# State-space stage of a two-block network: four groups one after the other, against three interleaved chains

## The reference

```
# 32 heads of 64 in 4 groups; sequence 512 in 4 chunks of 128; state size 128
cb      = C @ B^T                                  # once per group and chunk
decay   = exp(a_cum[l] - a_cum[s]), causal         # per head
y_diag  = (cb * decay) @ (x * dt)                  # "own" chunk
states  = B^T @ (x * dt * decay_to_end)            # per group and chunk, carried on
y_off   = (C @ state_before) * exp(a_cum)          # "past" chunks
y       = y_diag + y_off + d_skip * x
y       = rmsnorm_per_group(y * silu(z)) * gain    # over the 512 channels of a group
merged  = sigmoid(g_att) * (att @ w_att_out) + sigmoid(g_ssm) * (y @ w_ssm_out)
x       = x + merged @ w_out
```

## Time and profile before

| | |
|---|---|
| median of 3 runs | 2856.41 us (2852.3 to 2861.36) |
| the profiled execution | 2849.98 us, of which 2848.2 us is the span |
| granted TensorE clock over the span | 0.962 of full |
| PE busy | 2662.3 us (93%) |
| DVE, ACT, POOL busy | 1448.1, 663.1, 1142.3 us |
| state-space stage | 2050.46 to 2412.64 us, 362.2 us |

### The profile page before, as it was taken

The page is one execution under the profiler, slowest core; times in us unless marked ns, Lnnn a source line. Parts: engine busy times, 40 slices in busy tenths (PEclk is TensorE's granted clock), DMA queues, the critical chain, the costliest instruction groups (busy, mean ns, idle before and its releaser), DMA issues.

```text
span 2848.2 us, 30951 instructions
## 1 busy us (share of the span) xinstructions
PE 2662.3 (93%) x11724; PEld 2070.7 (73%) x11724; DVE 1448.1 (51%) x1985; ACT 663.1 (23%) x1297; POOL 1142.3 (40%) x764
## 2 busy tenths in 40 slices
PE   8999899999999999999999999999888778899998
PEld 6888688888666578888876777766555546688886
DVE  4754574565544435546566744544334447555521
ACT  2004420111233312102132133322213232222200
POOL 4333355555312145555544533322222113455554
PEclk9999999999899999999999999999888879999999
DMA  6433465656312156565644744434433214465565
GB/s 200 125 115 123 129 192 194 193 194 195 122 60 76 43 167 190 194 195 189 210 156 152 229 148 154 157 126 133 159 123 117 96 45 140 146 195 194 191 195 168
DMA packets 148857, 436.62 MB, mean 153 GB/s; under 512 B 13872, under 2 KB 18160, under 8 KB 148720
## 3 DMA queue, kind: packets, MB, share of 16 engines
q1 hardware_dynamic: 64224, 200.29, 23.9%
q0 software_dynamic: 67584, 201.35, 20.2%
q10 hardware_dynamic: 16912, 33.14, 3.2%
HBM read 417.90 MB, written 16.83 MB: 153 GB/s over the span
## 4 chain that ended last, share of the span: by engine, by line
issue 38%; PE 32%; POOL 23%; DVE 3%; DMA 2%; ACT 2%; DVEq 1%; ACTq 0%; POOLq 0%; SPq 0%
POOL w_lo L450 18%; PE bank L502 9%; PE bank L504 8%; PE bank L505 8%; POOL w_hi L432 5%; PE bank L703 1%; DMA projections<-spill_out 1%; PE bank L1117 1%; PE bank L777 0%; PE bank L780 0%; PE bank L779 0%; DMA residual<-x_in 0%; PE bank L1077 0%; DVE next_gained L2234 0%; PE bank L1107 0%
## 5 line engine op out<-in xcount | busy, mean ns | idle before, releaser
L450 POOL TENSOR_TENSOR w_lo<-w_raw,w_hi 128x1024 fp32r<-128x1024 f32 x376 | 908.9, 2418 | 15.1 <-DMA w_hi<-stream 7.1
L432 POOL DMA_DIRECT2D w_hi<-stream x376 | 227.2, 604 | 1673.1 <-PE bank L502 1505.4
L502 PE MATMUL bank<-x_hi,w_hi 128*128 128x512 f32 x1472 | 590.5, 401 | 26.8 <-POOL w_lo L450 13.5
L504 PE MATMUL bank<-x_lo,w_hi 128*128 128x512 f32 x1472 | 578.6, 393 | 0.0
L505 PE MATMUL bank<-x_hi,w_lo 128*128 128x512 f32 x1472 | 578.0, 393 | 0.0
L502 PEld LDWEIGHTS bank<-x_hi,w_hi 128*128 128x128 f32 x1472 | 279.8, 190 | 96.9 <-issue 20.9
L505 PEld LDWEIGHTS bank<-x_hi,w_lo 128*128 128x128 f32 x1472 | 279.6, 190 | 59.7
L504 PEld LDWEIGHTS bank<-x_lo,w_hi 128*128 128x128 f32 x1472 | 279.9, 190 | 57.5 <-issue 2.4
L1983 DVE TENSOR_TENSOR relu_sq<-relu 128x512 f32<-128x512 f32 x64 | 179.1, 2799 | 94.6 <-ACT relu L1395 94.6
L502 PE MATMUL bank<-hidden_hi,w_hi 128*128 128x512 f32 x512 | 199.2, 389 | 0.0
L504 PE MATMUL bank<-hidden_lo,w_hi 128*128 128x512 f32 x512 | 199.2, 389 | 0.0
(11 more groups left out here) (435 smaller groups left out, 4450.8 us busy)
## 6 DMA issues: line engine op xcount, KB each, us to landing
w_hi<-stream POOLq DMA_DIRECT2D x376, 512.0 KB, 4.8
w_raw<-stream SPq DMA_DIRECT2D x376, 512.0 KB, 3.7
projections<-spill_out ACTq DMA_DIRECT2D x56, 256.0 KB, 2.0
ssm_x<-projections ACTq DMA_DIRECT2D x4, 1024.0 KB, 7.2
gate_tiles<-projections ACTq DMA_DIRECT2D x16, 256.0 KB, 3.2
ssm_z<-projections ACTq DMA_DIRECT2D x4, 1024.0 KB, 9.5
residual<-x_in SPq DMA_DIRECT2D x4, 512.0 KB, 10.7
toeplitz_hi<-toeplitz_rows_hi POOLq DMA_DIRECT2D x4, 512.0 KB, 6.5
```

The source lines that it names most:

```text
L432: e.dma_start(in_slot(whi, t % SLOTS, o), in_stream(o)).then_inc(hi_ready[t % SLOTS], 16)
L450: e.tensor_tensor(wlo[:, s, :], raw[:, s, :], whi[:, s, :].bitcast(F32), ALU.subtract).then_inc(lo_ready, 1)
L502: mm = e.matmul(out, wh, rh, start=first, stop=False)
L504: e.matmul(out, wh, rl, start=False, stop=False)
```

## The change

The slots are replaced by one loop over the 16 head pairs in which three chains lie side by side on each engine: the pair itself; the preparation of the next group (`PREP_AT`: transposes T0 to T2 in pair 1, T3, B and the first state S0 in pair 2, S1 and S2 in pair 3); and the end of the group in front with its output units (`E_UNITS`, keys (g, p, place 1 to 3)). Only group 0 is prepared on its own ("first"). For that, `ssm_x_nat`, the states and B's copy are doubled, y has a buffer of its own, exp of the decay rows, y's high half, z and the gates have fewer buffers. x of group 0 is loaded some steps before the projections end. No arithmetic is added or removed.

```diff
@@ placing
+HEAD_STEPS = [(g, p) for g in range(4) for p in range(4)]
+PREP = ["T0", "T1", "T2", "T3", "B", "S0", "S1", "S2"]
+PREP_AT = {1: ["T0", "T1", "T2"], 2: ["T3", "B", "S0"], 3: ["S1", "S2"]}
...
+        ("first", 0): "a0", ("first", 3): "a1", ("first", 6): "a2",
+        (0, 0, 1): "a3", (0, 1, 1): "a4", (0, 2, 1): "a5", (0, 3, 1): "a6", (1, 0, 1): "a7",
+        (1, 2, 2): "o00", (1, 2, 3): "o01", (1, 3, 1): "o02", (1, 3, 2): "o03 o04", (2, 0, 1): "o05 o06",
+        (2, 0, 2): "o07",
...
+        ("last", 0): "o24 o25", ("last", 1): "o26 o27", ("last", 2): "o30 o31 o32 o33 o34 o35 o36 o37"}.items():
@@ PE
+                for g, p in HEAD_STEPS:
+                    n = 4 * g + p
+                    tasks = (PREP_AT.get(p, []) if g < 3 else []) + [None] * 3
+                    rows(n)
+                    units(g, p, 1)
+                    if tasks[0]:
+                        prep(g + 1, tasks[0])
+                    decay_rows(n)
+                    units(g, p, 2)
+                    if tasks[1]:
+                        prep(g + 1, tasks[1])
+                    own_past(n)
+                    if p == 3 and g < 3:
+                        products(g + 1)
+                    if p == 0 and g:
+                        squares_sum(g - 1)
+                    if tasks[2]:
+                        prep(g + 1, tasks[2])
+                    units(g, p, 3)
...
+                            if g == 1:
+                                e.wait_ge(e_add, 3)
+                            elif g:
+                                e.wait_ge(y_rstd, g - 1)
+                        for t in range(4):
+                            mm = e.transpose(bank[4][:, chunk(t)], sx[g % 2][:, t, chunk(c)], ident)
@@ ACT
+                    if n == 61:
+                        e.wait_ge(at_s, n0 + 48)
...
+                        load_x(0)
...
+                for g, p in HEAD_STEPS:
+                    n = 4 * g + p
+                    exponentials(n)
+                    if p == 0 and 1 <= g < 3:
+                        e.wait_ge(sg_yd, 4 * g)
+                        load_x(g + 1)
+                    units(g, p, 1)
+                    if p == 1 and g:
+                        root(g - 1)
+                    past_decay(n)
+                    units(g, p, 2)
+                    if n:
+                        square(n - 1)
+                        if n < 15:
+                            load_z(n + 1)
+                    if p == 2 and g < 3:
+                        natural_b(g + 1)
+                    units(g, p, 3)
+                    if p == 1 and g:
+                        his(g - 1)
@@ DVE
+                    if n:
+                        take_y(n - 1)
+                        gate_y(n - 1)
+                    if p == 2 and g:
+                        low_y(g - 1)
+                    decayed(n)
+                    units(g, p, 1)
+                    if tasks[0]:
+                        prep(g + 1, tasks[0])
+                    units(g, p, 2)
+                    if tasks[1]:
+                        prep(g + 1, tasks[1])
+                    if n:
+                        sum_y(n - 1)
+                    if tasks[2]:
+                        prep(g + 1, tasks[2])
+                    units(g, p, 3)
+                    if p == 1 and g:
+                        norm_y(g - 1)
```

More of the change, by code:

```diff
@@ L1137, in state_space, with units, rows @@
             def state_space():
-                def units(g, name):
-                    for x in E_STEPS[g, name]:
+                def units(*key):
+                    for x in E_UNITS.get(key, []):
                         unit(UNIT_AT[x])
[L1142 to L1159, removed]
+                def rows(n):
                     if n:
@@ new lines, in products, with squares_sum @@
+                def products(g):
+                    for c in range(ST):
+                        mm = e.matmul(bank[5][:, chunk(c)], sb[g % 2][:, chunk(c)], sc[g % 2][:, chunk(c)],
+                                      start=True, stop=True)
+                    mm.then_inc(e_cb, 1)
+                def squares_sum(g):
+                    e.wait_ge(y_sum, 3 * g + 3)
+                    if g < 3:
+                        e.wait_ge(e_add, 3 * (g + 1) + 3)
+                    else:
+                        e.wait_ge(y_rstd, 3)
+                    e.matmul(bank[4][:, :], ones, ysum[:, :], start=True, stop=True).then_inc(y_full, 1)
@@ new lines, in state_space @@
+                for i, task in enumerate(PREP):
+                    prep(0, task)
+                    if i == 0:
+                        products(0)
+                    units("first", i)
+                for g, p in HEAD_STEPS:
[17 more added lines that the diff above has]
+                    units(g, p, 3)
@@ L1234, in state_space @@
+                units("last", 0)
+                squares_sum(3)
+                units("last", 1)
+                units("last", 2)
                 f = flow["w_out"]
@@ new lines, in root, with his @@
+                def root(g):
+                    e.wait_ge(y_full, g + 1)
+                    e.activation(grs[:, :], bank[4][:, :], ACT.Ln, scale=0.25 / 512, bias=col("eps"))
+                    e.drain()
+                    e.activation(grs[:, :], grs[:, :], ACT.Exp, scale=-0.5).then_inc(y_rstd, 1)
+                def his(g):
+                    e.wait_ge(un_full, UNIT_AT["o", g - 1, 7] + 1 if g else UNIT_AT["a", 0, 7] + 1)
+                    for k in range(4):
+                        e.wait_ge(y_n, 4 * g + k + 1)
+                        e.activation(yh[:, k, :], yy[g % 2][:, k, :], ACT.Copy).then_inc(y_hi, 1)
@@ new lines, in state_space @@
+                for k in range(2):
+                    load_z(k)
+                for i, task in enumerate(PREP):
+                    if task == "B":
+                        natural_b(0)
+                    units("first", i)
+                for g, p in HEAD_STEPS:
[18 more added lines that the diff above has]
+                        his(g - 1)
@@ L1707, in state_space @@
+                square(15)
+                units("last", 0)
+                root(3)
+                units("last", 1)
+                his(3)
+                units("last", 2)
                 for m in range(8):
@@ L2300, in by_head, with units, take_y @@
                     return x.rearrange("p (n d) -> p n d", d=64)
[L2302 to L2303 removed]
+                def units(*key):
+                    for x in E_UNITS.get(key, []):
                         unit(UNIT_AT[x])
[L2306 to L2308 removed]
+                def take_y(n):
+                    g, p = n // 4, n % 4
+                    y = yy[g % 2][:, p, :]
@@ L2427, in state_space @@
+                take_y(15)
+                gate_y(15)
+                sum_y(15)
+                units("last", 0)
+                norm_y(3)
+                units("last", 1)
+                low_y(3)
                 for m in range(9):
```

413 lines of the change are left out of this document (161 added, 252 removed), and 9 rows, old and new, of tables (E_STEPS, E_UNITS).

## The result

| | before | after |
|---|---|---|
| median | 2856.20 us of 4 runs (2852.3 to 2861.36) | 2793.14 us of 4 runs (2792.05 to 2795.99) |
| ratio, 95% interval | | 0.978, 0.9762 to 0.9797 |
| profiled execution, span | 2849.98, 2848.2 us | 2793.69, 2791.9 us |
| granted TensorE clock over the span | 0.962 | 0.970 |
| state-space stage | 362.18 us | 301.27 us |

The forecast was 2790, range 2762 to 2824, with 300 us for the stage. The span shrank by 56.3 us and the stage by 60.9; after the stage nothing moved (435.56 and 435.28 us). Ahead of it 4.9 us were lost: the stage starts at 2055.35 instead of 2050.46. So I take the 4.9 us for the scatter of single executions, and compare stages by their own length.

What follows compares the result with a forecast made beforehand. The stage was taken as bound by PE and what keeps it waiting. Stretches summing to 296.3 us plus 4 contention made 300 instead of 362; 62 off 2849.98 gave 2788, forecast 2790 us, range 2762 to 2824.

Steps and rivals of the forecast that it cites:

- preparation of group 0: Start of the stage, three a units: 29.3 us, including 1.8 for one half-clock stretch after the S1 wait.
- group 1: Its four pairs: 60.6 us, with pair 1 held by the root and pair 2 by the norms.
- group 2: Its four pairs: 62.6 us, like group 1 but with pair 0 at 13.9 us for three units.
- tail: End of the stage: 44.2 us instead of 49.36, the 6.18 us wait shrinking to 3.8.
- contention: DVE operations delayed beside POOL's `w_lo`: perhaps 7 of 19 outside the tail meet one, half covered, +4 us.
- The half clock behind the root: Pair 1 of groups 1 and 2: after 6.4 us idle PE runs at half clock, 16.1 us instead of 12.9.
- Two signs: Pair 2 of groups 1 and 2: PE waits for `y_lo` and `ssm_g`; 5 of its 17.0 us idle.
- gate transfers: Tail, two gate buffers instead of three: landing 3.2 us after issue, inside two turns of 2.7, costed at nothing.
- The clock holds: Rival, chance 0.15: stretches between waits are dense enough for full clock, 14 to 20 us better, 2770.
- The clock stays low: Rival, chance 0.15: PE at 1.2 GHz through pairs 1, 2 and the first 5 us of pair 3, 2818.
- It doesn't interleave: Rival, chance 0.05: preparation tasks waiting for DVE hold up the in-order queue, 60 us, no change, 2850.
- POOL shuts DVE out: Rival, chance 0.05: `w_lo` meetings at 2.6 us each block DVE and eat the gain, up to 2878.

Runs made afterwards that it cites:

- warm_root: The changed kernel with 24 unused matmuls added on PE behind the rows of pair 1 of groups 1 to 3, during the root wait: 2784.96 us.
- serial_prep: The changed kernel with all eight preparation tasks of the next group in one row behind pair 3: 2828.63 us.
- late_serial: The changed kernel with x of group 0 loaded late and the next group's preparation in one piece behind pair 3: 2841.29 us.
- norms_early: root_first plus, on DVE, the four norms ahead of `decayed` in pair 1 and the low halves moved from pair 2 into pair 1: 2774.2 us.
- root_first: The changed kernel with the root ahead of the exponentials of pair 1 on ACT instead of behind them: 2781.61 us.
- norms_again: norms_early repeated unchanged, as base beside a version with ten added matmuls: 2774.22 us.

## Why the prediction was right

| stretch | predicted | measured |
|---|---|---|
| preparation of group 0 | 29.3 | 30.36 |
| group 0, pairs | 11.0, 12.0, 12.4, 14.3 = 49.7 | 11.05, 12.23, 12.65, 14.76 = 50.7 |
| group 1 | 11.9, 16.1, 17.0, 15.6 = 60.6 | 11.89, 15.16, 18.31, 15.72 = 61.1 |
| group 2 | 13.9, 16.1, 17.0, 15.6 = 62.6 | 14.35, 15.78, 17.06, 15.72 = 62.9 |
| group 3 | 13.9, 12.6, 13.1, 10.3 = 49.9 | 13.97, 12.55, 14.16, 10.3 = 51.0 |
| tail | 44.2 | 45.25 |
| contention | 4 | no rise counted |
| stage | 300 | 301.3 |

**The mechanism held, pair by pair.** Walking PE through the new order found every large wait: 6.34 us for the root (6.4), 2.64 for `take_y` with `decay_rows` at 5.3 us of pair 2 (5.5), o00 at 6.8 (6.9), pairs 0 and 3 with units covering what DVE and ACT do, at full clock (pair 3 without idle time; pair 0 of group 1 with one wait of 0.78). The half clock behind the root was right too, and warm_root priced it. Two signs were wrong in pair 2: no wait for `ssm_g`, and 3.2 and 3.3 us of idle time instead of 5. The 5 do not follow from the prediction's own times either, which leave about 3.5 (from the end of T3 to 5.5, and from the end of `decay_rows` to 6.9).

**Small terms that were off.** In the preparation T2 waited 1.92 us where 0.8 was forecast, since DVE was held by a0's eviction:

```profile
2063.17 0.69 DVE L2176 SCALAR_TENSOR_TENSOR merged<-gate_tiles,bank 128x512 f32<-128x512 f32 x1 [5.49 <-DMA gate_tiles<-projections]
2064.00 0.69 DVE L2396 TENSOR_TENSOR ssm_x_nat<-bank,ssm_dt 128x512 f32<-128x512 f32 x1
```

DVE had finished `ssm_x_nat` of T0 at 2057.7 and stood in its queue until the first gate landed; T1's copy was queued behind it, and PE waited for that. The 1.8 us of half clock that were forecast behind the wait of S1 came behind T2 and T3 in this execution, and in the six other traces not at all: there the preparation is 0.7 us under the forecast, so the 1.8 us, a guess from the earlier trace rows, were right here by luck. I had costed gate transfers at nothing by looking at PE's turns, not at what stands behind them on DVE. In group 1, o00 ran at 1.2 GHz to its last matmul, where I had let the clock come back midway: 18.31 instead of 17.0, while in group 2 it did come back midway and 17.0 became 17.06. The tail, PE in order of time:

```profile
2317.94 1.12 PE L1194 MATMUL bank<-y_square_sum,consts 128*128 128x512 f32 x2 [0.93 <-DVE y_square_sum L2368]
...
2327.21 0.47 PE L507 MATMUL bank<-y_hi,w_hi 128*128 128x512 f32 x1 [2.68 <-DVE ssm_out_sum L2182]
```

o30 starts 15.8 us after the last own products (15.6 forecast); the wait is 2.68 and not 3.8 only because a wait of 0.93 for the sum of squares came before it. The rest, from o30 to `w_out`, is 29.4 instead of 28.5.

**The term that failed is contention.** It is the step "perhaps 7 of 19 `w_lo` outside the tail meet one": +4 us, and twice as many long operations. Operations of DVE over 2.5 us in the stage number 6 before and 6 after, 4 of them in the tail both times. So outside the tail 2 had met a `w_lo` before, not the 3 of the prediction, and 2 did after. The term does not follow from its own numbers either: 4 more meetings of 2.6 us, half of them covered, are 5.2 us and not 4. One of the two outside the tail, on DVE and on POOL:

```profile
2125.13 3.02 DVE L2357 TENSOR_TENSOR ssm_y<-ssm_y,ssm_z 128x512 f32<-128x512 f32 x1
```

```profile
2125.17 2.41 POOL L455 TENSOR_TENSOR w_lo<-w_raw,w_hi 128x1024 fp32r<-128x1024 f32 x1
```

This one, too, ends only after POOL's has, as in the earlier trace rows, but denser work brought no more such meetings: the nine traces of the new orders have 5 to 7 in the stage. Why not was not tried. The six stretches came out 5.0 us over their sum of 296.3, and the 4 us put down for contention hid that: the stage is right to 1.3 us by two errors of opposite sign, and that it is so close is luck. The profiled execution came out at 2793.69 against 2788: 4.9 of that is the later start of the stage, 1.1 the stage itself (60.9 us saved, not 62).

**The rivals.** "The clock holds" is refuted by the half clock behind both waits for the root. Its price, 14 to 20 us in the same order, was not tested as a whole: keeping PE at work in pair 1 alone gave 6.5 to 7. "The clock stays low" into pair 3 did not come: pair 3 of groups 1 and 2 is 15.7 us in every version that has its tasks in it. "It doesn't interleave" is refuted by serial_prep, where the tasks in one row cost 35 us more. "POOL shuts DVE out" by the count.

**Where the 63 us come from.** The early load 9, the preparation spread over the pairs 35, together 44; late_serial leaves 15 to the placing of units, the end of the group in front and the buffers, and the 4 between depend on which part is taken out first. How the 15 divide was not tried.

## What to carry to other kernels

Walk the engine that bounds the stage through the new order one wait at a time, with start-to-start times at the clock that the waits allow: it gave each of 16 pairs within 1.4 us, where the sum of PE's work at full clock would have given 234 us for a stage of 301. When chains are interleaved, spread what has many short hand-overs (the preparation: 35 us) and look on every other engine for the operation that a bounded engine waits for behind work nobody waits for; two such moves, the root ahead of the exponentials and the norms ahead of `decayed`, gave another 19 us (2774 against 2793, with nothing added). A stage that looks right in sum should still be checked term by term, since here a rise of contention that did not come covered six small misses.

## What the runs showed of the hardware that was not expected

- PE can be nearly full and at half speed. In norms_early it was busy 18.0 of 20.47 us at a granted clock of 0.51, after waits of 0.67 and 2.47 us, in two executions at the same place. The prediction went by the 4.26 us of the earlier trace rows, but the earlier trace rows has the half clock already behind a wait of 2.93 us (own products 1.97). What PE did before the clock fell: own and past products, the sum of squares and six decay rows without a gap from 2140.28 to 2145.27, at 2.4 GHz, then the wait of 0.67. Ten independent matmuls there brought 2.4 GHz back for the own products. The page "TensorE: Matmul & The Clock Gate" of the Trainium skill (Part 1: The HAM clock gate) lays the clock to how busy PE has been recently; this trace shows a stretch 88% busy by its records, and the clock low throughout.
- The root takes two table loads of 1.28 us each, in all versions. The Trainium skill, "ScalarE: Activation LUTs" (Table sets: the hidden batching unit), says that a logarithm and an exponential share a set and need one load; the trace differs: a load stands ahead of each of the two activations. Which set each load takes the records don't say, so whether one would do is not shown. A load needs no data, so ahead of a wait it is free (2144.88 in root_first, in ACT's idle time), and behind the exponentials it is not (2152.77 in the change).
- The spans of single executions differ by 7 us ahead of the stage in code that is the same in all of them (2048.2 to 2055.7), which is more than most of the terms above; the five runs of norms_again, one kernel, spread over 9.8 us. Stretches in which PE is full repeat to 0.01 us (pair 3 of group 1: 15.72 or 15.73 wherever its tasks are spread).
